# A three-mixer language-model kernel: state-space segments from cumulative sums, a new home for the exponentials, and dt in channel layout

## The reference

```
z, xbc, dt = split(u @ w_in)          # 2048, 4096 and 64 columns
xbc = silu(dwconv(xbc, conv_w, conv_b))   # five taps; then xh (32 heads x 64), bm, cm (8 groups x 128)
dt = softplus(dt + dt_bias)           # two directions x 32 heads
a = -exp(a_log)
...
# ssd_scan, one direction, chunks of 128 tokens
cum = cumsum(dt * a)                  # within a chunk
decay = exp(where(causal, cum[l] - cum[s], -inf))
xdt = xc * dt
cb = einsum('blgn,bsgn->blsg', cc, bc)
y = einsum('blsgr,bsgrp->blgrp', cb * decay, xdt)
y = y + einsum('blgn,bgrpn->blgrp', cc, state) * exp(cum)
tail = exp(cum[-1] - cum)
state = state * exp(cum[-1]) + einsum('bsgn,bsgrp->bgrpn', bc, xdt * tail)
...
y = ssd_scan(forward) + reversed(ssd_scan(reversed inputs)) + xh * d_skip
y = rmsnorm(y * silu(z), per group) @ w_out
```

## Time and profile before

| what | value |
|---|---|
| median of 3 runs | 2245.17 us (2243.57 to 2246.26) |
| the profiled execution, time | 2246.52 us |
| its span, first to last instruction | 2244.8 us |
| mean granted TensorE clock | 0.977 |
| TensorE busy | 2152.3 us, 96% |
| VectorE busy | 974.1 us, 43% |
| ScalarE busy | 828.6 us, 37% |
| GpSimd busy | 909.4 us, 41% |

### The profile page before, as it was taken

One profiled execution on the slowest core, in us unless ns is written; L12 is line 12 of the kernel. 1 busy time (PEld: TensorE's weight loads), 2 busy tenths in 40 slices (PEclk: granted clock), 3 DMA queues, 4 the chain that ended last, 5 costly groups with the idle time before them and its releaser, 6 DMA issues.

```text
span 2244.8 us, 27334 instructions
## 1 busy us (share of the span) xinstructions
PE 2152.3 (96%) x10885; PEld 1744.7 (78%) x10885; DVE 974.1 (43%) x1435; ACT 828.6 (37%) x1312; POOL 909.4 (41%) x359
## 2 busy tenths in 40 slices
PE   7999999999999989999999999999989989999898
PEld 5878888888777778888888778888868776866676
DVE  3184433423334345333332777766761244452321
ACT  3123222122344342222222555555662154353332
POOL 3444444444423134444441666666654331221232
PEclk9999999999999999999997999999989999999999
DMA  4223332233332122332332211221213321111221
GB/s 152 96 76 104 110 97 94 77 98 107 104 94 76 57 75 94 94 100 89 91 96 62 58 56 57 58 75 57 57 38 94 98 76 38 57 57 38 57 73 59
DMA packets 233292, 176.56 MB, mean 79 GB/s; under 512 B 8531, under 2 KB 230023, under 8 KB 233176
## 3 DMA queue, kind: packets, MB, share of 16 engines
q1 hardware_dynamic: 230048, 174.13, 25.7%
q10 hardware_dynamic: 3128, 0.79, 0.2%
HBM read 172.75 MB, written 2.14 MB: 78 GB/s over the span
## 4 chain that ended last, share of the span: by engine, by line
PE 57%; issue 30%; POOL 8%; DVE 3%; ACT 2%; POOLq 0%; DMA 0%; ACTq 0%; DVEq 0%
PE bank L1690 16%; PE bank L1692 15%; PE bank L1691 15%; POOL wlo L530 7%; PE bank L2063 2%; PE bank L2260 1%; PE bank L2242 1%; PE bank L2111 1%; PE bank L2107 1%; PE bank L2256 1%; PE bank L2077 1%; PE bank L2224 0%; PE bank L2042 0%; PE bank L2268 0%; POOL P L553 0%
## 5 line engine op out<-in xcount | busy, mean ns | idle before, releaser
L530 POOL TENSOR_TENSOR wlo<-raw,whi 128x2048 fp32r<-128x2048 f32 (+1 forms) x168 | 737.7, 4391 | 1233.2 <-ACT whi L608 1233.2
L1690 PE MATMUL bank<-hHi,whi 128*128 128x512 f32 x1408 | 562.3, 399 | 4.0 <-DVE qk L1296 1.5
L1692 PE MATMUL bank<-hHi,wlo 128*128 128x512 f32 x1408 | 549.4, 390 | 0.0
L1691 PE MATMUL bank<-hLo,whi 128*128 128x512 f32 x1408 | 548.9, 390 | 0.0
L608 ACT ACTIVATE whi<-raw 128x2048 fp32r<-128x2048 f32 (+1 forms) x168 | 304.0, 1810 | 474.9 <-PE bank L1692 473.7
L1690 PEld LDWEIGHTS bank<-hHi,whi 128*128 128x128 f32 x1408 | 265.0, 188 | 69.1 <-issue 12.2
L1691 PEld LDWEIGHTS bank<-hLo,whi 128*128 128x128 f32 x1408 | 265.1, 188 | 59.4 <-issue 5.7
L1692 PEld LDWEIGHTS bank<-hHi,wlo 128*128 128x128 f32 x1408 | 264.7, 188 | 56.4
L1690 PE MATMUL bank<-whi,hHi 128*128 128x256 f32 x896 | 260.2, 290 | 5.9 <-ACT lg L1031 3.9
L1691 PE MATMUL bank<-wlo,hHi 128*128 128x256 f32 x896 | 255.9, 286 | 0.0
L1692 PE MATMUL bank<-whi,hLo 128*128 128x256 f32 x896 | 255.7, 285 | 0.0
(11 more groups left out here) (328 smaller groups left out, 3168.9 us busy)
## 6 DMA issues: line engine op xcount, KB each, us to landing
raw<-in_ssd_w_in SPq DMA_DIRECT2D x48, 512.0 KB, 4.8
raw<-in_ffn_w_gate SPq DMA_DIRECT2D x44, 512.0 KB, 4.5
raw<-in_ffn_w_up SPq DMA_DIRECT2D x44, 512.0 KB, 4.8
raw<-in_gla_w_in SPq DMA_DIRECT2D x40, 512.0 KB, 4.5
raw<-in_conv_w_in SPq DMA_DIRECT2D x24, 512.0 KB, 4.4
raw<-in_ffn_w_down SPq DMA_DIRECT2D x32, 384.0 KB, 3.6
raw<-in_attn_w_qkv SPq DMA_DIRECT2D x24, 512.0 KB, 4.4
raw<-in_ffn_w_down SPq DMA_DIRECT2D x32, 320.0 KB, 4.0
```

Of the source, the lines that this page charges most:

```text
L530: pool.tensor_tensor(wlo[s][:, 0:w], raw[s][:, 0:w], whi[s][:, 0:w].bitcast(F32), ALU.subtract).then_inc(w_lo, 1)
L1690: pe.matmul(dst, hi1, hi2, start=first, stop=False)
L1691: pe.matmul(dst, hi1, lo2, start=False, stop=False)
L1692: return pe.matmul(dst, lo1, hi2, start=False, stop=last)
```

## The change

- The cumulative sums are made in channel layout (64 rows, direction and head, by 512 tokens): dt is one product with 512 columns (24 matmuls), softplus and decay run on 64 partitions, VectorE scans. Sums in a high and a low part go to DRAM (`cums`) and come back for each group as rows (`decay_rows`), ten a chunk: in U two rows with the high and low sums of the four heads side by side and eight rows that are -1 over one head, in L two rows of ones and the eight rows of sums. ScalarE copies them to fp32r once a group (`rows`).
- `segments` is two fp32r products of ten rows, 512 columns, forward in one bank (FB) and backward in another (BB). ScalarE copies BB to SBUF (`back_out`), VectorE takes the minimum of the two into FB (`least`), ScalarE writes the exponential to MT in SBUF, and GpSimd multiplies MT by its coupling, inside `coupled`. `mix` and `segment_rows` are gone.
- dt, the exponentials of the sums and the tails are turned to token layout by TensorE (`to_tokens`); the 24 small products are gone. The dt product stands behind `project(0, 1)` instead of ahead of it; `project(1, 0)` stands ahead of group 0.
- The scaling of xT is one tile a group (two in group 6) behind `gate(g, 1)`. Five low parts of y are made inside the last group, and the output projection's first column runs over 14 k-steps before the last transposes.
- GpSimd writes constant rows to DRAM at the kernel's start (`pick_rows`).

```diff
@@ SP @@
+                def decay_rows(g):
+                    if g:
+                        sp.wait_ge(S("rows_ready"), 4 * g)
+                    for d in range(2):
+                        at = (SSD_HEADS * d + HPG * g) * 2 * SEQ
+                        U, L = (m_ssd[f"{n}in{d}"] for n in "UL")
+                        for r in range(2):
+                            src = bass.AP(tensor=cums.tensor, offset=at + SEQ * r, ap=[[P, NT], [2 * SEQ, HPG], [1, P]])
+                            sp.dma_start(U[r::32, :].rearrange("c (h e) -> c h e", h=HPG), src).then_inc(S("rows_in"), 16)
+                        for c in range(NT):
+                            src = bass.AP(tensor=cums.tensor, offset=at + P * c, ap=[[SEQ, 2 * HPG], [1, P]])
+                            sp.dma_start(L[32 * c + 2:32 * c + 2 + 2 * HPG, :], src).then_inc(S("rows_in"), 16)
+                    if n == 1:
+                        picks()
+                    elif n == 3:
+                        cums_out()
+                        decay_rows(0)
+                    elif kind == "bc" and g:
+                        decay_rows(g)
@@ GpSimd @@
                 pool.tensor_tensor(coupling(n), coupling(n), acc[:, :], ALU.add).then_inc(S("p_ready"), 1)
+                pool.wait_ge(S("p_ready"), n + 1)
+                pool.wait_ge(S("ex_ready"), n + 1)
+                pool.tensor_tensor(weights(n), weights(n), coupling(n), ALU.mult).then_inc(S("mt_ready"), 1)
+                coupled(NT * g)
+                if g != 1:
+                    unit_low(UNIT_OF["z", max(g - 1, 0)] + 2)
+                coupled(NT * g + 1)
                 if g:
                     pool.wait_ge(S("gated"), 2 * g)
                 for c in range(NT):
                     pool.tensor_tensor(h4(chunk("ybuf", c)), h4(chunk("xt", c)), bc(m["dsk"][:, HPG * g:HPG * (g + 1)], 64), ALU.mult)\
                         .then_inc(S("skip_ready"), 1)
-                coupled(NT * g)
-                if g != 1:
-                    unit_low(UNIT_OF["z", max(g - 1, 0)] + 2)
-                coupled(NT * g + 1)
@@ ScalarE @@
-                def segment_rows(n):
...
+                def rows(g):
+                    act.wait_ge(S("rows_in"), 192 * (g + 1))
+                    for d in range(2):
+                        for name in (f"U{d}", f"L{d}"):
+                            copy(m[name][:, :], m[f"{name[0]}in{d}"][:, :], S("rows_ready"))
+                def back_out(n):
+                    act.wait_ge(S("seg"), n + 1)
+                    if n:
+                        act.wait_ge(S("seg_least"), n)
+                    if n >= NT and n % NT == 0:
+                        act.wait_ge(S("y_squared"), n)
+                    copy(m["back"][:, :], BB[:, :], S("back_ready"))
                 def exponential(n):
-                    act.wait_ge(S("seg"), n + 1)
-                    act.activation(seg_bank(n)[:, :], seg_bank(n)[:, :], ACT.Exp).then_inc(S("ex_ready"), 1)
+                    act.wait_ge(S("seg_least"), n + 1)
+                    if n >= 3:
+                        act.wait_ge(S("y_mm"), n - 2)
+                    act.activation(weights(n), FB[:, :], ACT.Exp).then_inc(S("ex_ready"), 1)
@@ VectorE @@
-                def mix(n):
-                    dve.wait_ge(S("ex_ready"), n + 1)
-                    dve.wait_ge(S("p_ready"), n + 1)
-                    if n >= 3:
-                        dve.wait_ge(S("y_mm"), n - 2)
-                    tt(weights(n), seg_bank(n)[:, :], coupling(n), ALU.mult).then_inc(S("mt_ready"), 1)
+                def least(n):
+                    dve.wait_ge(S("back_ready"), n + 1)
+                    tt(FB[:, :], FB[:, :], m["back"][:, :], ALU.min).then_inc(S("seg_least"), 1)
+                    least(n)
                     if more:
                         taps(g + 1, 0)
-                    mix(n)
+                    least(n + 1)
                     states(g)
                     if more:
                         taps(g + 1, 1)
-                    mix(n + 1)
+                    else:
+                        for k in range(3):
+                            y_low(k)
+                    least(n + 2)
+                taps(0, 0)
+                dve.wait_ge(S("dt_log"), 1)
+                chain(ts(dtT, dtT, hcol[:, 0:1], 0.0, ALU.add, ALU.max))
+                chain(tt(dtT, dtT, tmp, ALU.add))
+                dve.wait_ge(S("decay_exp"), 1)
+                chain(ts(laT, dtT, hcol[:, 1:2], -1.0, ALU.mult, ALU.mult))
+                for d in range(2):
+                    way = slice(None, None, -1 if d else 1)
+                    chain(dve.tensor_tensor_scan(dirs_of(cum)[d][:, way], dirs_of(again)[d], dirs_of(laT)[d][:, way], 0.0, ALU.mult, ALU.add))
...
+                for q in range(1, 4):
                     taps(0, q)
@@ TensorE @@
                 project(0, 0, normed=MID)
                 sums(MID)
+                project(0, 1)
                 pe.wait_ge(S("wdt_ready"), 1)
-                for c in range(NT):
-                    for k in range(KT):
-                        x = slice(SEQ * k + P * c, SEQ * k + P * (c + 1))
-                        w = slice(64 * k, 64 * k + 64)
-                        ins = product(bank[4][:, 64 * c:64 * c + 64], hHi[:, x], hLo[:, x], m["wdtHi"][:, w], m["wdtLo"][:, w], k == 0, k == KT - 1)
+                for k in range(KT):
+                    x, w = slice(SEQ * k, SEQ * (k + 1)), slice(DTH * k, DTH * (k + 1))
+                    ins = product(bank[4][0:DTH, :], m["wdtHi"][:, w], m["wdtLo"][:, w], hHi[:, x], hLo[:, x], k == 0, k == KT - 1)
                 ins.then_inc(S("dt_mm"), 1)
-                project(0, 1)
@@ TensorE, segments @@
-                    pe.wait_ge(S("rm_ready"), 8 * n + 8)
-                    if n >= 2:
-                        pe.wait_ge(S("mt_ready"), n - 1)
-                    for d, mat in enumerate((GT, LT)):
-                        ins = pe.matmul(seg_bank(c)[:, :], mat[:, :], rows(n, d), start=(d == 0), stop=(d == 1))
+                    if c == 0:
+                        pe.wait_ge(S("rows_ready"), 4 * g + 4)
+                        if g > 1:
+                            pe.wait_ge(S("sz_ready"), NT * g)
+                    if n:
+                        pe.wait_ge(S("ex_ready"), n)
+                    at = slice(32 * c, 32 * c + 2 + 2 * HPG)
+                    for d, dst in enumerate((FB, BB)):
+                        ins = pe.matmul(dst[:, :], m[f"L{d}"][at, :], m[f"U{d}"][at, :], start=True, stop=True)
                     ins.then_inc(S("seg"), 1)
@@ TensorE, order @@
+                    chunk_out(g, 0)
                     segments(g, 3)
-                    chunk_out(g, 0)
...
+                project(1, 0)
+                pe.wait_ge(S("decay_kept"), 5)
                 for g in range(SSD_GROUPS):
                     group(g)
```

More of the change, by code:

```diff
@@ L363, in coupling, with headed, dirs_of, last_of @@
             return m_ssd[("P0", "P1")[n % 2]][:, :]
[L365 to L370, removed]
+        FB, BB = bank[2], bank[3]
+        DTH = 2 * SSD_HEADS
+        def headed(name, k=0):
+            return m_ssd[name][0:DTH, SEQ * k:SEQ * (k + 1)]
+        def dirs_of(ap):
+            return (ap[0:SSD_HEADS], ap[SSD_HEADS:DTH])
+        def last_of(ap, d):
+            at = (P - 1) * (1 - d)
+            return v3(dirs_of(ap)[d], NT)[:, :, at:at + 1]
         def in_bank(g, q):
@@ L911, in group @@
                         group_root(g - 1)
-                    exponential(NT * g)
-                    segment_rows(NT * g + 2)
+                    back_out(NT * g)
                     if g != 1:
                         unit_high(UNIT_OF["z", max(g - 1, 0)] + 2)
+                    exponential(NT * g)
+                    if not more:
+                        act.wait_ge(S("cb_mm"), SSD_GROUPS)
+                        for k in range(3):
+                            y_hi(k)
                     if g:
                         turned_out(g - 1, 0)
+                    back_out(NT * g + 1)
                     exponential(NT * g + 1)
-                    segment_rows(NT * g + 3)
+                    if not more:
+                        act.wait_ge(S("rows_ready"), 4 * SSD_GROUPS)
+                        for k in range(3, 5):
+                            y_hi(k)
                     if more:
@@ L926, in group @@
                         z_silu(g, 1)
+                    back_out(NT * g + 2)
                     exponential(NT * g + 2)
-                    if more:
-                        segment_rows(NT * g + 4)
+                    back_out(NT * g + 3)
                     exponential(NT * g + 3)
                     if more:
-                        segment_rows(NT * g + 5)
-                    if more:
+                        rows(g + 1)
                         for q in range(3):
@@ L940, in group @@
                     else:
-                        for k in range(7):
+                        ahead(U_SSD_OUT, 0, 0)
```

(32 more changed lines are left out.)

207 lines of the change are left out of this document (119 added, 88 removed).

## The result

The changed kernel takes 2196.24 us (median of 4 runs, 2195.67 to 2197.22) against 2245.48 for the kernel before on the same chip: a ratio of 0.9782, 95% interval 0.9765 to 0.9799, 49.2 us less. The forecast was 2190.5 us with a range of 2177 to 2211. The profiled execution took 2197.22 us, its span was 2195.5 (2244.8 before) and the mean granted clock 0.979.

A forecast was written before the change was run, and what follows sets the result against it. TensorE's own queue was taken to set the pace, except at both stage ends. Start and group 0 (24.1), groups 1 to 6 (27.3) and end (3.3) sum to 54.7 us won: 2190.5 us, range 2177 to 2211.

The forecast's parts named there:

- Segments: Segment products in the state-space stage: two ten-row fp32r products cost 0.45 us a chunk, not 1.72, saving 5.07 a group.
- rival 1: Segment products: ten-row products cost a full fp32 pass (0.43 us each), 13.1 us less won, 2203.6 us; chance 0.09.
- Will the group follow?: Middle groups: other engines keep up with slack 0.7 us; net saving 4.55 us a group, 27.3 for groups 1 to 6.
- what would show it: Expected trace signs, among them middle groups of 47.0 to 47.5 us and, without slack, the fourth segment product awaiting its exponential.
- The start: Start of the state-space stage: group 0 begins at 1245.2 instead of 1259.1, 13.9 us won, with VectorE deciding.
- Rival 4: Stage start and group 0: VectorE isn't blocked and group 0 has few waits, 11 us more won, 2179.5 us; chance 0.15.
- Group 0: First group of the stage: about 39 us instead of 49.2, 10.2 shorter, 5.5 of it the moved projection.
- The end: Last group to first output column: 51.6 us instead of 54.9, 3.3 won; without early low parts GpSimd's delay costs 4.
- The kernel's start: Before the first projection: GpSimd's added steps of some 8 us stay hidden by loading x; otherwise some 2 us.
- the first sentence: Opening of the prediction: only the state-space stage is read, since the diff otherwise touches a few instructions at the kernel's start.
- 2: VectorE's chain late in every group, GpSimd blocking states and scaling: 18 us less won, 2208.7 us; chance 0.17.
- 3 to 5: 3: GpSimd's queue delays splits, 2256 us, chance 0.05; 4: see Rival 4; 5: segments save nothing, 2225 us, chance 0.05.

The follow-up runs named there:

- e2: The changed kernel with g45 back at 8 elements a partition, all else as changed: 2208.93 us, ratio 0.9834.
- e8: The changed kernel with left segment matrices in zero-padded blocks, so each segment product runs over all 128 rows with right numbers: 2188.27 us, ratio 0.9748.
- e5: The changed kernel with the product of exponential and coupling moved from GpSimd back to VectorE in all groups: 2219.54 us, ratio 0.9890.
- e7: The changed kernel with two GpSimd weight splits moved: group 0's end one into group 1, the last group's behind its fourth coupling: 2191.77 us, ratio 0.9763.
- e6: The changed kernel with the five early low parts of y put back behind the last group: 2196.13 us, ratio 0.9782.
- e11: The changed kernel with the product of exponential and coupling on VectorE in the last group alone: 2195.78 us, ratio 0.9776.
- e10: The changed kernel with only the last group's splits moved: first behind the fourth coupling, second held until all of sLo is written: 2199.47 us, ratio 0.9792.
- e12: The changed kernel with e8's blocks, e7's group 0 and e10's last group, but second split waiting only for VectorE's last gate, g45 at 64 bytes: 2188.58 us.

## Why the prediction was right, and where it was not

The time fell inside the range, 5.7 us above the forecast, but two errors stand against each other: 16 us too much was expected of the stage, and 11 to 13 us of addresses were not seen at all. That the sum came so near is luck. By its mechanisms alone the kernel would have come out near 2209 us, the median of e2, still within the range but only just.

- **Segments (term 0.45 us a chunk).** Mis-sized: 0.85, at the other bound of that term (0.86) and so the price of rival 1. But it is not the fp32 pass by which that bound was set: it was assumed that the number of rows changes nothing, and e8 showed that a part of the rows costs 0.38 to 0.40 us a pair. Over groups 1 to 6 that is 9.6 us; 3.0 of it comes back in the next step, and with 0.5 more that group 1 gained, 6.0 of the 16 us are here.
- **Will the group follow?** Right, and the slack was as thin as said. TensorE waits for nobody in a middle group, so the 0.5 us allowed for a short wait wasn't taken, but only because the dearer pairs bring TensorE later to the fourth one. In e8, with pairs near the forecast's price, the fourth segment product waits 0.16 us for the exponential, as "what would show it" had it, and the group takes 47.42 us, where the step had 47.5. e5 showed the same thinness from the other side. I had not priced what the product's move to GpSimd is worth: 23 us, since left on VectorE it would have broken the chain in every group.
- **The start (13.9 us).** Right: 14.13, with TensorE idle for 3.9 us ahead of group 1's projection (forecast 4.4), released by VectorE's taps, and VectorE's dt step took 4.98 us beside the z split, as forecast. The transfers through DRAM lay hidden. Rival 4 didn't come.
- **Group 0 (near 39 us).** Mis-sized by 4.8 us, and the step's own terms don't add up: 34.2 us of work and waits of 1, 1, 1, 2 and 3 us are 42.2, not 39. Measured are 33.5 us busy and 10.3 of waits. GpSimd's last product came at 35.4 us, earlier than the 37.0 forecast. What failed is the sentence that collection releases group 1 at about 39. GpSimd's next split starts right behind that product and holds two of VectorE's sums for 4.87 us, and the wait at the end is 5.9 us instead of 3. e7 took the split away and had 39.79 us.
- **The end (3.3 us won).** Wrong in sign, 2.2 lost. The last GpSimd product started at 35.7 us (1610.63), not 32.6. GpSimd works there without a break from 1576.80 on: its four products took 5.6 us in sum where the step had 4.2, the four skip products 3.66 us, and a coupling up to 2.1 us for a half, where the undisturbed ones take 1.04. And the early low parts, which were to make up for it, are worth 0.6 us (e6). The granted clock was also lower, 0.84 against 0.88; what that costs here was not taken apart. Taking work from GpSimd did bring the last product earlier (e7, e11), and each time a split then held VectorE. So the two engines bound the end together. What a good order of them is stays open: four were tried (e7, e10, e11, e12) and none gained over 0.6 us without a loss beside it.
- **The kernel's start (0).** Right within what runs vary (20.1 to 21.8 us over fourteen profiles): the first split ended at 17.8 us (forecast 16.5), ahead of the first product at 21.8.
- **The unchanged stages (not in the sum).** The step that failed is the first sentence, that the diff touches nothing but the state-space stage and a few instructions at the start. One of its lines resizes a tile.
- **Rivals.** 1 came true in its price, by another cause; a held VectorE as in 2 showed in group 0 and at the end, but not in the middle groups; 3 to 5 did not come.

## What to carry to other kernels

Read a diff's allocations as part of it: a tile that changes size moves all that is allocated behind it, and a kernel that TensorE bounds feels where its operands lie. When an operation must be beside a long one of GpSimd's, look for every VectorE sum with both inputs in SBUF within the next 5 us, not just at the load of the engines; a split of 4.6 us is best put where VectorE reads PSUM (beside one, the mixing product from a bank kept its 0.68 us) or where nobody waits for it (e7's group 1). And a product over ten rows can cost more than one over all 128; where zero blocks are cheap, give it all rows. When a change makes one engine quicker, look at the next wait in each place: of four equal savings a group, e8 kept three.

## What the runs showed of the hardware that was not expected

- TensorE's pace hangs on the SBUF addresses of its moving operand. By the tiles' sizes, everything allocated ahead of g45 is a multiple of 256 bytes a partition. With g45 at 32 bytes the f0aHi products are recorded at 396 ns and 176 k-steps take 122.5 us; at 64 bytes 392 to 394 (but f0aLo's 388), and 120.1 us; at 256 bytes 389, and 119.0 us. Over this kernel it is 11 to 13 us, 0.5%. Since at 64 bytes the high and the low part differ, the offset from a multiple of 256 isn't all of it. The mechanism was not looked into.
- Pairs of fp32r products over ten or 32 rows, put among products over all rows, cost the same, and over 128 rows 0.38 to 0.40 us less, half of it ahead of the pair and half behind it.
- Two VectorE sums of 0.89 us together take 4.87 beside one GpSimd split, and moving the split often only chose another victim (e7's last group, e11, e12).
